# First q, k, v: rows turned one product sooner, last q tile behind the first scores; dilated head reordered, closing rows tile by tile

## What is computed

```python
def attn_mixer(h_lat, h_ctx, w_qkv, q_g, k_g, w_o, cos, sin, ctx_out):
    qkv = h_lat @ w_qkv
    q = rmsnorm(qkv[..., :Q_DIM].reshape(B, S, N_Q_HEADS, HEAD_DIM), q_g)
    ...
    q = apply_rope(q, cos, sin)
    k = apply_rope(k, cos, sin)
    kv_c = h_ctx @ w_qkv[:, Q_DIM:]
    ...
        s = jnp.einsum('bqhgd,bkhd->bhgqk', q_blk, k_all).astype(jnp.float32)
        p = jax.nn.softmax(s, axis=-1).astype(v_all.dtype)
        return jnp.einsum('bhgqk,bkhd->bqhgd', p, v_all)

def dilated_attention(xn, w_qkv, w_o, rel_bias):
    qkv = (xn @ w_qkv).reshape(B, S, 3, G, Hg, dh)
    for g, (window, dilation) in enumerate(DIL_GROUPS):
        o, lse = strided_window_attention(qkv[:, :, 0, g], qkv[:, :, 1, g], qkv[:, :, 2, g],
        ...
    wts = jax.nn.softmax(jnp.stack(lses), axis=0)
    ...
    return o @ w_o

def second_block(...):
    for i in range(DEPTH):
        ...
        x = x + rms_norm(m, norm_gains[i, 1])
        ...
        x = x + rms_norm(f, norm_gains[i, 3])
```

## Time and profile before

| | us |
|---|---|
| median of three runs (lowest to highest) | 2203.86 (2203.27 to 2206.57) |
| the profiled execution, its own time | 2203.53 |
| its span, from the first to the last instruction | 2202.2 |
| PE busy | 2090.0 (95%) |
| VectorE busy | 1288.9 (59%) |
| ScalarE busy | 1038.1 (47%) |
| TensorE's granted clock, mean | 0.976 of full speed |

### The profile page before, as it was taken

The page is one execution under the profiler, slowest core; times in us unless marked ns, Lnnn a source line. Parts: engine busy times, 40 slices in busy tenths (PEclk is TensorE's granted clock), DMA queues, the critical chain, the costliest instruction groups (busy, mean ns, idle before and its releaser), DMA issues.

```text
span 2202.2 us, 31215 instructions
## 1 busy us (share of the span) xinstructions
PE 2090.0 (95%) x13108; PEld 1661.7 (75%) x13108; DVE 1288.9 (59%) x1935; ACT 1038.1 (47%) x1572; POOL 127.4 (6%) x106
## 2 busy tenths in 40 slices
PE   5979988999996998999999999999999999999998
PEld 4666666777775665788788888888877778888887
DVE  3467767766647775355646666534245556766633
ACT  3546634355635664377845433324244345433322
POOL 0012213100011220000000000000000000000000
PEclk9989999999997999999999999999999999999999
DMA  9999980123227995211213323223222213223220
GB/s 397 375 361 371 382 329 1 44 111 116 103 85 270 355 360 212 102 62 39 77 39 115 112 80 115 86 96 103 83 93 67 87 49 112 105 90 115 77 105 39
DMA packets 40812, 325.89 MB, mean 148 GB/s; under 512 B 7343, under 2 KB 8495, under 8 KB 21935
## 3 DMA queue, kind: packets, MB, share of 16 engines
q1 hardware_dynamic: 28008, 290.68, 34.6%
q0 software_dynamic: 11200, 27.80, 3.7%
q10 hardware_dynamic: 1456, 5.32, 0.6%
HBM read 312.17 MB, written 24.19 MB: 153 GB/s over the span
## 4 chain that ended last, share of the span: by engine, by line
PE 89%; DVE 4%; ACT 3%; issue 2%; DMA 2%; SPq 0%; DVEq 0%; ACTq 0%; POOLq 0%
PE PS L166 82%; PE PS L998 2%; PE PS L745 1%; DMA work<-tokens,slots 1%; PE PS L1349 1%; PE PS L865 1%; PE PS L1109 0%; DMA work<-in_xtok 0%; DVE work L2703 0%; DVE work L2632 0%; ACT work L1825 0%; PE PS L881 0%; ACT XH L1475 0%; DMA ring<-ys 0%; DVE XL L2099 0%
## 5 line engine op out<-in xcount | busy, mean ns | idle before, releaser
L166 PE MATMUL PS<-HS,RS 128*128 128x512 f32 (+1 forms) x3248 | 727.8, 383 | 2.5 <-DVE RS L2006 2.5
L166 PEld LDWEIGHTS PS<-HS,RS 128*128 128x128 f32 x3248 | 595.9, 188 | 122.8 <-DVE RS L2006 2.7
L2006 DVE TENSOR_TENSOR RS<-ring,RS 128x1024 fp32r<-128x1024 f32 x201 | 246.1, 1227 | 310.8 <-ACT RS L1433 310.8
L1433 ACT ACTIVATE RS<-ring 128x1024 fp32r<-128x1024 f32 x201 | 209.8, 1051 | 259.5 <-PE PS L166 259.5
L166 PE MATMUL PS<-RS,HS 128*128 128x512 f32 x1344 | 307.6, 390 | 3.1 <-DVE HS L2361 2.7
L166 PEld LDWEIGHTS PS<-RS,HS 128*128 128x128 f32 x1344 | 251.6, 188 | 56.2 <-issue 2.2
L1937 ACT ACTIVATE work<-work,vec 128x512 f32<-128x512 f32 x88 | 71.8, 816 | 240.0 <-DVE work L2768 240.0
L2006 DVE TENSOR_TENSOR CR<-ring,WR 128x1024 fp32r<-128x1024 f32 x128 | 153.2, 1221 | 36.2 <-ACT WR L1433 33.3
L1433 ACT ACTIVATE WR<-ring 128x1024 fp32r<-128x1024 f32 x139 | 145.7, 1056 | 52.9 <-PE PS L166 45.2
L166 PE MATMUL PS<-work 128*64 128x128 f32 (+5 forms) x1728 | 133.1, 295 | 26.8 <-DVE work L2065 19.5
L166 PEld LDWEIGHTS PS<-work 128*64 128x64 f32 (+2 forms) x1728 | 108.2, 148 | 47.5 <-issue 31.4
(11 more groups left out here) (312 smaller groups left out, 2839.2 us busy)
## 6 DMA issues: line engine op xcount, KB each, us to landing
ring<-in_wexp SPq DMA_DIRECT2D x32, 2048.0 KB, 10.8
ring<-in_wmod SPq DMA_DIRECT2D x24, 2048.0 KB, 11.3
ring<-in_ffnu SPq DMA_DIRECT2D x22, 2048.0 KB, 7.6
ring<-in_wexp SPq DMA_DIRECT2D x32, 1024.0 KB, 11.1
ring<-in_ffnd SPq DMA_DIRECT2D x10, 2048.0 KB, 7.2
ring<-in_dilqk SPq DMA_DIRECT2D x6, 2048.0 KB, 7.6
ring<-in_sbqk SPq DMA_DIRECT2D x4, 2048.0 KB, 7.5
ring<-in_dilv SPq DMA_DIRECT2D x3, 2048.0 KB, 7.7
```

Of the source, the lines that this page charges most:

```text
L166: return T.matmul(out, l, r, start=start, stop=stop, skip_group_check=True)
L1433: return S.activation(out, x, ACT.Copy, **kw)
L2006: V.tensor_tensor(lo, src, hi.bitcast(F32), ALU.subtract).then_inc(w_lo, 1)
```

## The change

In the first attention: turns 0 and 1 move ahead of product 6, and turns 2 and 3 stand behind it; `scores(0)` moves up, behind product 12, then come turns 10 and 11 (in banks 6 and 7), product 13, and turn 12; turn 13 moves behind the four turns of pass 0. ScalarE does the two exponentials of pass 0 before the rows of tile 13, which takes two more table loads, and the copies of pass 0 before the exponentials of pass 1. VectorE's order follows. Product 13 counts once more, at its third k-step, since the first exponentials write over the inputs of its steps 0 to 2.

In the dilated attention: the q/k units 16 and 17 become 12 and 13, ahead of group 2's v (now 14 to 17). Their weights are loaded as two tiles of 1 MB in place of one of 2 MB. `scores(0)` stands in the middle of group 2's v. The part has four units split in advance, not three. Its close has apart = 3, with one more unit in spare room.

In all four closes: tile 3 is made bank by bank, and counts after its first bank. ScalarE and VectorE take the two halves of tile 3 one after the other, the first as soon as it is counted (in the last part), and VectorE reads a half only after ScalarE has squared it.

```diff
@@ pe_program, attention @@
             product(4, 5)
+            turned(0)
+            turned(1)
             product(6)
-            for j in range(4):
-                turned(j)
+            turned(2)
+            turned(3)
...
             product(12)
-            turned(10)
-            turned(11)
-            product(13)
-            turned(12)
...
+            pe.wait_ge(at_e, 10)
             scores(0)
+            turned(10)
+            turned(11)
+            product(13)
+            turned(12)
...
                 turn(u, 0)
                 turn(u, 1)
+                if u == 0:
+                    turned(13)
@@ act_program, attention @@
-            rows(13)
-            turned_hi(12)
...
+            act.wait_ge(at_p, 14)
             powers(0, 0)
             powers(0, 1)
+            table(0)
+            rows(13)
+            S.activation(tiny[:, 2:3], C("eps"), ACT.Exp)
+            turned_hi(12)
             for u in range(32):
...
+                if u == 0:
+                    turned(0, 0)
+                    turned(0, 1)
+                    turned_hi(13)
                 if u + 1 < 32:
                     powers(u + 1, 0)
                     powers(u + 1, 1)
@@ dve_program, attention @@
             most(0, 0)
             most(0, 1)
-            rows_done(13)
-            turned_lo(12)
+            rows_done(12)
+            turned_lo(10, 11)
+            rows_read(13)
             for u in range(32):
                 ada_quarter(u)
+                if u == 0:
+                    rows_done(13)
+                    turned_lo(12)
@@ streams @@
-    stream("dil", qk_units[:1] + [(("dilv", n), ..., 4) for n in range(3)] + qk_units[1:] +
+    stream("dil", qk_units[:1] + v_units[:2] + qk_half[:1] + v_units[2:] + qk_half[1:] + qk_units[2:] +
            [(("dilo", 0), A["dilo"], 4096, by_rows(4, 1024), 4)], 2, 2, 2, None, (2, 1),
-           (("ring", 4), ("work", 2048), ("work", 8192)), 6144)
+           (("ring", 4), ("work", 2048), ("work", 8192), ("work", 12288)), 6144)
+    DIL_V = (4, 8, 14)
@@ pe_program, dilated @@
+                else:
+                    pe.wait_ge(pr_c, 16)
+                    for i in range(2):
+                        project(first + 12 + i, i, 2)
+                    pe.wait_ge(pr_c, 20)
+                project_rows(first + DIL_V[g], 4 * min(g, 1), 2, between=(lambda: scores(0)) if g == 2 else None)
-            close(2, first + 36, 4, 2, ...
+            close(2, first + 36, 4, 3, ...
@@ close @@
             for t in range(4):
-                for k in range(kc - apart, kc):
-                    x = row_products(..., [b for b in (BANK[t], BANK[t] + 1) if (b, k) not in made])
+                for half_ in ((BANK[t], BANK[t] + 1),) if t < 3 else ((BANK[t],), (BANK[t] + 1,)):
+                    for k in range(kc - apart, kc):
+                        x = row_products(..., [b for b in half_ if (b, k) not in made])
@@ dve_program, out_gain @@
-            for h in (1, 0):
+            for h in (1, 0) if t < 3 else (0, 1):
...
-                if h == 0:
-                    dve.wait_ge(*rows_squared(a, "out", f"{t}0"))
+                if t == 3 and h:
+                    dve.wait_ge(*done)
+                if t == 3 or h == 0:
+                    dve.wait_ge(*rows_squared(a, "out", f"{t}{h}"))
```

More of the change, by code:

```diff
@@ L274, in build @@
     for n in range(2):
-        ring.place(("wq", n), A["wq"][n], 4096, (at_p, 4 * n + 10))
+        ring.place(("wq", n), A["wq"][n], 4096, (at_p, (10, 15)[n]))
     for c in range(2):
@@ L327, in parts @@
         before = first - over[n] if 0 <= n < places else p - places + 1
-        spare = SPARE.get(name, {})
+        spare, dead = SPARE.get(name, ({}, 0))
         home = spare.get(n)
@@ L340, in parts @@
             both = [spare_rows[:, home + x * 1024:home + x * 1024 + 1024] for x in range(2)]
-            before = first + min(spare) - places
+            before = first + dead
         elif n >= 0:
@@ L1077, in project, with project_rows @@
                 x.then_inc(w_done, 1)
-        def project_rows(first, b0, i, call=None, turns=((),) * 8):
+        def project_rows(first, b0, i, call=None, turns=((),) * 8, between=None):
             for q in range(4):
+                if between and q == 2:
+                    between()
                 key, src, hi, lo, before = parts(first + q)
@@ L1131, in close @@
             for t in range(4):
-                for k in range(kc - apart, kc):
[L1133 to L1137, removed]
+                for half_ in ((BANK[t], BANK[t] + 1),) if t < 3 else ((BANK[t],), (BANK[t] + 1,)):
+                    for k in range(kc - apart, kc):
+                        x = row_products(first + k, src, ready, k, kc, [b for b in half_ if (b, k) not in made])
+                        if half_[0] == BANK[3] + 1:
+                            x.then_inc(w_done, 1)
+                    if half_[0] != BANK[3] + 1:
+                        x.then_inc(ro_m, 1)
                 if t == 2 and a < 3:
@@ L1362, in values @@
                 x.then_inc(sm_pv, 1)
[L1364 to L1365 removed]
+            for g in range(3):
+                if g == 0:
+                    pe.wait_ge(rc_c, 2)
+                elif g == 1:
+                    pe.wait_ge(dq, 2)
+                    pe.wait_ge(dk, 2)
+                else:
[4 more added lines that the diff above has]
+                project_rows(first + DIL_V[g], 4 * min(g, 1), 2, between=(lambda: scores(0)) if g == 2 else None)
             for u in range(16):
@@ L1390, in free @@
                     pe.wait_ge(sm_n, 12)
-            close(2, first + 36, 4, 2, lambda k: (OT[0][:, k, :], OT[1][:, k, :]), lambda k: pe.wait_ge(f_l, 16 + k + 1), free,
+            close(2, first + 36, 4, 3, lambda k: (OT[0][:, k, :], OT[1][:, k, :]), lambda k: pe.wait_ge(f_l, 16 + k + 1), free,
                   (0, 1, 2, 3, 4, 5, 7, 6))
@@ L1902, in finish @@
                 copy(in_order(OT[0][:, p, :]), blocks(d_o)[:, :, ::-1]).then_inc(f_h, 1)
-            project_qk(0)
+            for i in range(12, 17):
+                split_hi("dil", ahead("dil", i))
             powers(0, 0)
             powers(0, 1)
+            project_rows("dil", DIL_V[2], lambda t: d_V[:, 2, t, :], 4, 2)
             for u in range(16):
@@ L2459, in turned_lo @@
                                     ALU.subtract).then_inc(sx_l, 1)
-            for j in range(7):
+            for j in range(6):
                 rows(j)
-            turned_lo(0, 1, 2, 3)
+            turned_lo(0, 1)
+            rows(6)
+            turned_lo(2, 3)
             rows(7)
@@ L2471, in attention @@
             turned_lo(8, 9)
-            rows(12)
-            turned_lo(10, 11)
-            rows_read(13)
+            rows_read(12)
             P, Tb, st, rl = soft(9728)
@@ L2715, in dilated @@
             qk_scaled(0, range(4, 6))
+            for i in range(14, 17):
+                split_lo("dil", ahead("dil", i))
             most(0, 0)
             most(0, 1)
+            project_rows("dil", DIL_V[2])
             for u in range(16):
```

102 lines of the change are left out of this document (46 added, 56 removed).

## The result

| | before | after |
|---|---|---|
| median (lowest to highest), us | 2206.57 (2203.27 to 2207.90), 5 runs | 2192.43 (2188.14 to 2195.12), 5 runs |
| profiled execution, its own time, us | 2203.53 | 2191.64 |
| its span, us | 2202.2 | 2190.3 |
| PE busy, us | 2090.0 | 2089.4 |

The ratio of the times is 0.9937 (95% interval 0.9920 to 0.9955), so the change takes off 13.9 us, with 9.9 and 17.7 as the ends. The forecast was 2187.3, its range 2184.4 to 2190.4: the kernel became faster, as forecast, and its time lies 2.0 us above the range. The page of after says where the time is still spent; its first line answers to the earlier trace rows.

The account below looks back on a forecast made before the run. PE, busy 95% of the span, bounds the kernel; only its idle time and halved clock can give time back. Terms 7.0 + 0.2 + 2.5 + 5.2 + 1.3 = 16.2 off 2203.5 give 2187.3 us, range 2184.4 to 2190.4.

Parts of the forecast that it names:

- A: First attention's turns one product sooner: the 4.28 us wait and the half clock behind it go, 7.0 us saved.
- B: First attention, first scores ahead of product 13: `scores(2)` 1.2 us sooner, less 1.0 for half clock, 0.2 us saved.
- C: Dilated part, one more unit split in advance: the 2.51 us wait for unit 3 goes, 2.5 us saved.
- D: Dilated head, `scores(0)` inside group 2's v: last projection to `scores(2)` falls from 11.4 to 6.2 us, 5.2 saved.
- E: Closes: the 1.33 us wait ahead of `turn_pair` in the dilated close goes, 1.3 us saved.
- the base: Whole kernel: the sum starts from the profiled execution's 2203.53 us, taken to match the median 2203.86 within 0.4 us.
- Rival 1: Part B's chain is longer, by table switch or load behind product 13's wait: B -1.5, 2189.0 us; chance 0.10.
- Rival 2: PE keeps its clock in pass 0 and the four turns flow: B +3, 2184.5 us; chance 0.06.
- rival 3: A weight unit is late in the dilated head: 3 to 4 us and perhaps the clock, 2191 us; chance 0.04.
- Bank by bank: Tile 3 at the kernel's end, one bank after the other: taken as 0, bounds -0.2 and +0.7 us.
- Rivals 4 and 5: 4: second experts eat attention's 7.2 us, 2194.5, chance 0.04. 5: first attention's 31 later passes slow, 2209, chance 0.02.

Follow-up runs that it names:

- before again: The kernel before, unedited, profiled again on another chip: 2208.05 us in its profiled execution, median 2207.94 us.
- before, third: The kernel before, unedited, profiled a third time on another chip: 2212.12 us in its profiled execution, median 2208.81 us.
- C, D, E alone: The changed kernel with the first attention as before, only the dilated head, fourth unit split in advance and closes changed: 2197.92 us, ratio 0.9943 to before.
- A alone: The kernel before with only turns 0 and 1 put ahead of product 6, splits in that order: 2204.13 us against 2209.67, ratio 0.9964.
- after without B: The changed kernel with the first scores put back behind product 13, all else changed: 2193.27 us, ratio 0.9923 to before.
- A and B: The kernel before with the whole first-attention change (turns sooner, first scores ahead of product 13), second block as before: 2204.00 us, ratio 0.9984 to before.
- after again: The changed kernel, unedited, timed and profiled again on another chip: 2191.25 us, ratio 0.9930 to before.
- after, third: The changed kernel, unedited, timed and profiled a third time on another chip: 2191.79 us, ratio 0.9928 to before.
- scores(0) behind v: The changed kernel with the first dilated scores put behind group 2's v, not in its middle: 2197.06 us, ratio 0.9950 to before.
- tile 3 in one go: The changed kernel with tile 3 of all four closes made in one piece again, as in before: 2194.15 us, ratio 0.9934 to before.
- the maxima first: The changed kernel with pass 1's maxima and exponentials moved earlier and turn 13 behind `scores(2)`: 2187.64 us, ratio 0.9910 to before; repeat 2190.75, ratio 0.9915.

## Why the prediction was wrong, and where it was right

| part | forecast | by stage lengths |
|---|---|---|
| A, turns | -7.0 | -6.9 (18.9 to 12.1) |
| B, scores ahead of product 13 | -0.2 | -0.4 (27.0 to 26.6) |
| C, unit 3 | -2.5 | -2.7 |
| D, dilated head | -5.2 | -5.3 |
| E, closes | -1.3 | -1.5 |
| sum | -16.2 | -16.8 |

A and B are cut at the work that the edits move: A from the end of product 5 to turn 4, B from the end of product 12 to `scores(3)`; "half" is the time at the granted 0.50 within them; us.

```
trace                     A      half    B      half
before                    19.1    6.8    24.9    6.8
before again              18.1    3.4    26.5   10.2
before, third             19.2    6.8    27.5   13.7
C, D, E alone             19.3    6.8    27.6   13.7
A alone                   12.1    0      27.7   10.2
after without B           12.1    0      27.6   13.7
A and B                   12.1    0      26.3   10.2
after                     12.1    0      26.9   10.2
after again               12.1    0      25.6    6.8
after, third              12.1    0      27.0   10.2
scores(0) behind v        12.1    0      27.0   10.2
tile 3 in one go          12.1    0      26.7   10.2
```

For A the 18.9 is the mean of the four traces with the old turns; for B the 27.0 is the mean of the six with the old order of the scores, the 26.6 that of the six with the new. The three timings of after give -13.9, -15.5 and -15.9 us, each with some 4 us of interval to either side. Over all chips the 43 runs of before have a mean of 2208.0 us and the 17 of after one of 2192.0, which is 16.0 apart. So the sum is right, and it is right term by term, not by errors that cancel.

**The step that failed is the base.** The prediction says that the profiled 2203.53 and the median 2203.86 "stand for the same within 0.4 us". Both came from the lower end of what this kernel does: the medians of before in the four comparisons are 2206.57, 2209.67, 2207.94 and 2208.81, single runs 2201 to 2213. Of the 5.1 us between 2187.3 and 2192.43, 3.0 are the base in this very comparison (2206.57 against 2203.53); the other 2.1 (14.1 us between the medians, not 16.2) lie within its interval of 9.9 to 17.7. The mean of before's three profiled executions is 2207.9 us, and less 16.2 that is 2191.7; the medians of after are 2192.43, 2191.25 and 2191.79. What the first trace lacked is mostly the 4 us in the second experts (282.6 against 286.5 and 286.9), where the clock was whole for 10 to 14 us longer, and some 2 us in pass 0 (24.9 in the table, against 26.5 and 27.5). The range failed with it: it takes in the forecast with two of its rivals and has nothing for the spread of one program from run to run, which is wider (12 us for before, 9 for after) than the range (6.0). The bounds of the terms, 8.9 to 20.7 us off, would have taken the result in. The last sentence, "I am wrong if a window elsewhere has changed length", named the place to look.

**A.** The wait is gone, product 7 takes 5.60 us, and nothing is awaited behind it: as forecast. Against the trace from which the term was taken the gain is 7.0 us, the forecast's own number; against "before again" it is 6.1, since there only 3.4 us behind the same wait were at half clock.

**B.** The order of events came as worked out: waits of 0.78, 3.15 and 1.44 us (forecast 0.6, 3.3, 2.0), the fourth turn 15.2 us behind product 12 (forecast 15.2). `scores(2)` came 19.4 us behind it (forecast 18.7). The missing 0.7 us are the half clock, which the prediction charged to `scores(2)` alone: in after it starts at 428.3, ahead of the fourth turn, and the turns on which ScalarE's copy and split wait are slow as well. In "after again" it starts only behind that turn, and `scores(2)` comes 18.8 us behind product 12:

```profile
430.23 0.55 PE L999 MATMUL PS<-cst,work 128*128 128x128 f32 x3 [3.15 <-DVE work L2504]
430.61 0.74 PE L935 MATMUL PS<-cst,ring 128*128 128x128 f32 x4
433.80 0.80 PE L166 MATMUL PS<-RS 64*128 64x512 f32 x2 [1.44 <-ACT work L1700]
```

The two turns take 0.55 and 0.74 us here, 0.90 and 1.06 in after; the waits are the same. Over six traces each, `scores(2)` comes 1.0 us sooner with the new order (forecast 1.2), and 0.4 of that is left at `scores(3)`. The single traces differ by more, so that B gains at all is not clear of the spread.

Rival 1 named a load behind the wait for product 13. That is not what happened: the load went out at 417.15, ahead of that step's end at 418.0. It stood behind the wait for the maxima, its price was 0.4 us at the first exponential and not 1.7, and the fourth turn was not late by it. The load took 1.28 us and the exponential began 1.30 us after its start. The Trainium skill, "ScalarE: Activation LUTs", "What ACT_TABLE_LOAD costs", counts a drain of 1.38 us on top; this trace, like the earlier trace rows, has none. Rival 2 (the clock stays whole) did not come in after; in one of the two traces of "the maxima first" it did.

**C, D, E.** As worked out, to 0.3 us each: no wait for unit 3, 1.10 us ahead of the first L1348 (forecast 1.0), 4.6 us behind the last projection (forecast 4.6), none ahead of `turn_pair`, no weight unit late (rival 3). Bank by bank is 0 (taken: 0; its bound of +0.7 can go). D's price of the old order, 5.2 us, hid how much of it rests on ScalarE's order: with the scores' place alone undone the head lost 6.9. How long the clock was halved in before's dilated head hardly mattered: 6.8, 3.4 and 6.8 us of it in the three traces, and 97.3 to 97.4 us each time. All three had `scores(1)` in it (2.93 us against 1.57 at the whole clock), and behind that `scores(2)` waited for VectorE whether the turns between were slow or not.

**Rivals 4 and 5.** The passes behind pass 2 take 156.2 us in before and after, so no pass became slower. The second experts don't take the attention's gain: with before's attention they last 282.6 and 286.5 to 286.9 us in four traces (mean 285.7), with after's 284.6 to 289.2 in six (mean 287.2), and in the two traces with the shortest attention of all, those with the maxima first, 282.4 and 288.0 us. A lengthening by 1 or 2 us is not ruled out by so few; the 7.2 of rival 4 are.

Still open: what sets the length of a half-clock stretch behind one and the same wait. No run here varied that alone.

## What to carry to other kernels

Sum the terms against the median of many runs, and give the range the spread of that median and of the clock stretches beside the bounds of the terms. If the profile is one execution, price an edit by stages cut at the same matmul, in more than one trace of each kernel: a stage that nobody touched tells what a difference is worth. Put the cuts where both orders have done the same work, ahead of all that moved and behind it. Where the first scores are pulled ahead of a projection, follow the orders of VectorE and ScalarE too, since what the next pass needs (maxima, exponentials, copies) must stand ahead of the last tile's closing work.

## What the chip showed unexpectedly

- The same program with the same waits spends different times at the granted 0.50: in the first attention's pass 0 6.8 to 13.7 us with before's order of the scores, in the second experts 34.1 to 54.6 us over all kernels. This goes with up to 2.7 and some 7 us of time, of 2200.
- Before the drop at 428.3 in after PE was busy 3.97 of 7.30 us; in the kernel with the maxima first 5.53 of 7.30, and the clock stayed at 1.00. In its repeat, with the same order and no wait above 1.50 us, 3.4 us at 0.50 came all the same.
- A table load goes out ahead of the last wait of its exponential: at 431.72 in before, ahead of the maxima; at 417.15 in after, behind the maxima and ahead of product 13's step; and with the dilated `scores(0)` behind v 13.3 us ahead of its exponential at 1620.25, so only the first of two waits can bring it onto the chain:

```profile
1606.91 1.28 ACT L1909 ACT_TABLE_LOAD   x1
```
